# State-space input tables: built by GpSimd in turned layout, beside attention

## The reference, cut to what matters

```python
# attention of the first mixer
p = softmax(concat(q_pos @ keys_lat, q_free @ keys_ctx) * scale)
o = p[..., :s] @ ckv_l + p[..., s:] @ ckv_c          # then @ w_uv, * silu(gate), @ w_out
# state space, one of two directions, 128 groups of 64 complex states and 16 channels
lam_bar = exp(lam * dt)
b_bar = ((lam_bar - 1.0) / lam)[..., None] * bmat
bu = einsum('btgs,gps->btgp', u, b_bar)              # input into the states
h[t] = lam_bar * h[t-1] + bu[t]                      # associative scan
y = einsum('btgp,gsp->btgs', h, cmat).real
# modulation of both blocks
sh, sc, gt = split(silu(c) @ w_mod[i] + b_mod[i], 3)
```

## Time and profile before

| what | value |
|---|---|
| time, median of 3 runs (lowest to highest) | 1574.73 us (1572.53 to 1574.93) |
| the profiled execution, span | 1571.2 us |
| PE busy | 1503.4 us, 96% of the span |
| PEld busy | 1129.3 us, 72% |
| DVE busy | 872.9 us, 56% |
| ACT busy | 402.3 us, 26% |
| POOL busy | 565.2 us, 36% |
| mean granted TensorE clock | 0.993 |

### The profile page before, as it was taken

One profiled execution on the slowest core, in us unless ns is written; L12 is line 12 of the kernel. 1 busy time (PEld: TensorE's weight loads), 2 busy tenths in 40 slices (PEclk: granted clock), 3 DMA queues, 4 the chain that ended last, 5 costly groups with the idle time before them and its releaser, 6 DMA issues.

```text
span 1571.2 us, 25477 instructions
## 1 busy us (share of the span) xinstructions
PE 1503.4 (96%) x10192; PEld 1129.3 (72%) x10192; DVE 872.9 (56%) x1745; ACT 402.3 (26%) x956; POOL 565.2 (36%) x412
## 2 busy tenths in 40 slices
PE   4999989999999999999998999999999999999998
PEld 3455555666655558898877888887788874688887
DVE  5979944554578978378466321243543422265642
ACT  1222243333311222322233011001223550232210
POOL 4013340000002314101002977773496301477774
PEclk9999999999999999999999999999999999999999
DMA  9856771050286646747666455445544133455441
GB/s 332 221 173 194 242 237 45 3 159 14 100 262 228 202 174 180 273 166 287 251 252 260 159 195 182 161 163 185 191 167 146 70 108 107 131 179 164 168 150 68
DMA packets 172605, 272.99 MB, mean 174 GB/s; under 512 B 51405, under 2 KB 85304, under 8 KB 171208
## 3 DMA queue, kind: packets, MB, share of 16 engines
q1 hardware_dynamic: 146096, 201.08, 38.1%
q0 software_dynamic: 16512, 42.49, 8.4%
q10 hardware_dynamic: 9880, 27.78, 4.8%
HBM read 228.26 MB, written 42.99 MB: 173 GB/s over the span
## 4 chain that ended last, share of the span: by engine, by line
PE 88%; DVE 5%; DMA 3%; issue 2%; ACT 2%; POOL 0%; DVEq 0%; ACTq 0%; POOLq 0%
PE bank L499 82%; PE bank L502 6%; DMA memory<-in_w_mod 1%; DMA memory<-mc_scratch 1%; DVE memory L2417 1%; DVE memory L2418 1%; DVE memory L2424 0%; DVE memory L2421 0%; DMA memory<-in_s_log_dt 0%; DVE memory L2574 0%; ACT memory L1514 0%; ACT memory L1386 0%; ACT memory L1738 0%; DVE memory L2445 0%; DVE memory L2444 0%
## 5 line engine op out<-in xcount | busy, mean ns | idle before, releaser
L499 PE MATMUL bank<-memory 128*128 128x256 f32 (+8 forms) x9244 | 1404.7, 355 | 40.4 <-issue 8.5
L499 PEld LDWEIGHTS bank<-memory 128*128 128x128 f32 (+4 forms) x9244 | 1022.3, 166 | 378.1 <-issue 250.1
L2783 POOL DMA_DIRECT2D mc_scratch<-memory x32 | 28.0, 874 | 505.5 <-DVE memory L2138 447.7
L502 PEld LDWEIGHTS bank<-memory 128*128 128x128 f32 (+1 forms) x948 | 109.3, 142 | 59.4 <-issue 33.6
L502 PE MATMUL bank<-memory 128*128 128x128 f32 (+1 forms) x948 | 125.9, 277 | 23.5 <-ACT memory L1358 8.6
L2822 POOL TENSOR_TENSOR memory<-memory 128x1024 f32<-128x1024 f32 (+1 forms) x34 | 80.9, 2378 | 143.5 <-PE bank L499 96.2
L2808 POOL DMA_DIRECT2D memory<-mc_scratch x32 | 17.3, 541 | 189.7 <-PE bank L499 189.7
L2824 POOL TENSOR_TENSOR memory<-memory 128x1024 f32<-128x1024 f32 (+1 forms) x34 | 80.9, 2380 | 2.7
L2789 POOL DMA_DIRECT2D k_scratch<-memory x128 | 76.2, 629 | 14.5 <-ACT memory L1431 14.1
L2827 POOL TENSOR_TENSOR memory<-memory 128x1024 f32<-128x1024 f32 (+1 forms) x34 | 80.0, 2353 | 2.7
L2825 POOL TENSOR_TENSOR memory<-memory 128x1024 f32<-128x1024 f32 (+1 forms) x34 | 80.4, 2366 | 0.0
(11 more groups left out here) (305 smaller groups left out, 1284.3 us busy)
## 6 DMA issues: line engine op xcount, KB each, us to landing
memory<-in_s_w_glu SPq DMA_DIRECT2D x32, 1024.0 KB, 7.5
memory<-in_w_mod SPq DMA_DIRECT2D x12, 2048.0 KB, 14.1
memory<-in_w_ffn_up SPq DMA_DIRECT2D x22, 1024.0 KB, 6.9
memory<-in_w_in SPq DMA_DIRECT2D x10, 2048.0 KB, 8.0
mc_scratch<-memory POOLq DMA_DIRECT2D x32, 512.0 KB, 4.5
mb_scratch<-memory ACTq DMA_DIRECT2D x32, 512.0 KB, 3.7
memory<-mb_scratch SPq DMA_DIRECT2D x32, 512.0 KB, 7.3
memory<-mc_scratch POOLq DMA_DIRECT2D x32, 512.0 KB, 6.5
```

The costliest lines, as they stand in the source:

```text
L499: return nc.tensor.matmul(o, l, r, start=start, stop=stop, skip_group_check=free)
L502: return nc.tensor.transpose(o, i, ident[0:n, 0:n])
L2783: pool.dma_start(mc_dram[u], over(mc[:, u % 3, GS:GS + 1], (144, 8), (1, P))).then_inc(*S.up("mc_out%d" % (u % 3), u, by=16))
```

## The change

1. The input table is no longer made by DVE and transposed by PE. PE transposes the raw `b` once for each quarter (`b_turned`, 4 times 8 transposes), ACT copies and stores it (`bt_scratch`); DVE makes rows of powers once (`power_rows`, some 40 small operations behind unit 2), POOL stores them (`pw_scratch`). Then POOL, for each of the 32 units, loads both spread over the partitions (`pair_load`, three DMAs) and multiplies (`mixed_unit`: two operations of 128x1024, two of 128x512, one store DMA). The unit's complex product is computed in turned layout, so nothing is transposed afterwards.
2. POOL starts once unit 15's output table and the modulation product (0, 5) are done. Its pairs live in ring slot 1; its results in the buffer `gtb` (units 0 to 26) and in the buffer of the probabilities (units 27 to 31, `LAST_MIXED`, after the last head).
3. `gate_rows(0)`, which writes `gtb`, moves behind attention, and on ACT waits for the stores of units 25 and 26.
4. The stores of the output tables and taps move from POOL to ACT.
5. The scaling of the probabilities moves from DVE to ACT (`norm`).
6. The second half of the query weights is loaded right behind the first; the six modulation loads of the second mixer share slot 2, their products stand in heads 8, 9, 11, 12, 14 and 15. The last output weights wait for the last mixed unit. `b` is loaded for all quarters in the gates; quarters 2 and 3 are saved and loaded again (`b_again`).

```diff
-MOD_AT = {3: 0, 5: 1, 10: 2, 12: 3}
+MOD_AT = {8: (1, 0), 9: (1, 1), 11: (1, 2), 12: (1, 3), 14: (1, 4), 15: (1, 5)}
+LAST_MIXED = 5
...
+        pairs = ring[:, 1, :].rearrange("p (a b n) -> p a b n", a=2, b=2)
+        mixed_b = (gtb, hT_flat[:, 0:2048].rearrange("p (a n) -> p a n", a=2))
...
@@ loads @@
+        uq_load(0, 2)
+        uq_load(1, 0)
+        for ct in range(6):
+            mod_load(1, ct, 2)
...
@@ PE @@
-            def unit_turned(u):
-                pe.wait_ge(*S.at("mb", u))
-                for dr in range(2):
-                    b = bank(pe, ("mbT", u, dr), [("mbt", (u, dr))], 4 + dr)
-                    for i in range(4):
-                        last = tr(b[:, i * P:(i + 1) * P], mb[:, u % 2, dr * 512 + i * P:dr * 512 + (i + 1) * P])
-                    last.then_inc(*S.up("mbT_mm", (u, dr)))
-                if u % 2:
-                    kernels(u // 2)
+            def b_turned(q, i):
+                pe.wait_ge(*S.at("b_load%d" % (q % 2), q))
+                for ql in range(2):
+                    b = bank(pe, ("bT", q, ql), [("bT", (q, ql))], i + ql)
+                    for n in range(4):
+                        c = (n % 2) * 512 + (n // 2) * 256 + ql * P
+                        last = tr(b[:, n * P:(n + 1) * P], b_loaded(q)[:, c:c + P])
+                    last.then_inc(*S.up("bT_mm", (q, ql)))
...
             mod_turned(0, 5, 7)
-            gate_rows(0)
-            unit_turned(15)
+            kernels(7)
...
@@ PE, behind the last head @@
-            mod_product(1, 4)
-            mod_product(1, 5)
-            mod_turned(1, 4)
-            mod_turned(1, 5)
+            gate_rows(0)
...
@@ ACT, unit_stored @@
-                for dr in range(2):
-                    act.wait_ge(*S.at("mbT_mm", (u, dr)))
...
-                    A(mbt_(u)[:, dr * 512:(dr + 1) * 512], at_bank("mbT", u, dr), ACT.Copy).then_inc(*S.up("mbt", (u, dr)))
-                act.wait_ge(*S.at("mbt", (u, 1)))
-                act.dma_start(mb_dram[u], mbt_(u)).then_inc(*S.up("mbt_out%d" % (u % 2), u, by=16))
+                act.wait_ge(*S.at("mc", u))
+                act.dma_start(mc_dram[u], over(mc[:, u % 3, GS:GS + 1], (144, 8), (1, P))).then_inc(*S.up("mc_out%d" % (u % 3), u, by=16))
...
+                    for j in range(L):
...
+                        act.dma_start(to, kt[:, kp % 2, (7 - j) * GS:(7 - j) * GS + P]).then_inc(*S.up("k_out%d" % (kp % 2), kp, by=16))
...
@@ ACT, attention @@
+            def norm(h):
+                c = 4 * (h % 2)
+                act.wait_ge(*S.at("inverse", h))
+                for t in range(NTT):
+                    act.wait_ge(*S.at("p", (h, t)))
+                    o = pl[:, h % 2, t, :] if t < 2 else pc[:, h % 2, t - 2, :]
+                    A(o, o, ACT.Copy, scale=st0[:, 56 + c + t:57 + c + t]).then_inc(*S.up("pn", (h, t)))
...
@@ ACT, behind the last head and six DMA issues @@
+            for u in (NU - LAST_MIXED - 2, NU - LAST_MIXED - 1):
+                act.wait_ge(*S.at("mb_out%d" % (u % 2), u))
+            gate_rows(0)
             for ql in range(2):
                 c_conjugated(2, ql)
...
@@ DVE, unit: the six operations of the input table @@
-                tt(o[0], w[0], b[0], ALU.mult).then_inc(*S.up("unit_op", (u, 5)))
...
-                tt(o[1], o[1], t[1], ALU.add).then_inc(*S.up("mb", u))
...
@@ POOL @@
+            def pair_load(u):
+                q, g8 = u // 8, u % 8
+                if u >= 2:
+                    pool.wait_ge(*S.at("mixed", u - 2))
+                b, w = pairs[:, u % 2, 0, :], pairs[:, u % 2, 1, :]
+                pool.dma_start(b, dview(bt_dram, q * P * 8 * P + g8 * GS * 8 * P, (0, 8), (8 * P, GS), (1, 8 * P))).then_inc(*S.up("pair_in%d" % (u % 2), u, by=16))
+                for ql in range(2):
+                    src = dview(pw_dram, (16 * q + 8 * ql + g8) * 4096, (512, 8), (0, GS), (1, 512))
+                    pool.dma_start(w[:, ql * 512:(ql + 1) * 512], src).then_inc(*S.up("pair_in%d" % (u % 2), u, by=16))
+            def mixed_unit(u):
...
+                pool.wait_ge(*S.at("pair_in%d" % (u % 2), u))
+                if u >= 2:
+                    pool.wait_ge(*S.at("mb_out%d" % (u % 2), u - 2))
+                if u == NU - LAST_MIXED:
+                    pool.wait_ge(*S.at("pt_mm", (H - 1, 2)))
+                nc.gpsimd.tensor_tensor(both(o), both(b), both(w, 0, 0), ALU.mult).then_inc(*S.up("mix_op", (u, 0)))
+                pool.wait_ge(*S.at("mix_op", (u, 0)))
+                nc.gpsimd.tensor_tensor(both(w), both(b, P, -P), both(w, P, 0), ALU.mult).then_inc(*S.up("mix_op", (u, 1)))
+                pool.wait_ge(*S.at("mix_op", (u, 1)))
+                nc.gpsimd.tensor_tensor(part(o, 0), part(o, 0), part(w, 0), ALU.subtract).then_inc(*S.up("mix_op", (u, 2)))
+                nc.gpsimd.tensor_tensor(part(o, P), part(o, P), part(w, P), ALU.add).then_inc(*S.up("mixed", u))
+                pool.wait_ge(*S.at("mixed", u))
+                pool.dma_start(mb_dram[u], o).then_inc(*S.up("mb_out%d" % (u % 2), u, by=16))
+            pool.wait_ge(*S.at("mod_mm", (0, 5)))
+            pool.wait_ge(*S.at("mc", 15))
+            pool.wait_ge(*S.at("pw_out"))
+            for u in range(NU + 1):
+                if u < NU:
...
+                    pair_load(u)
+                if u:
+                    mixed_unit(u - 1)
```

255 lines of the change are left out of this document (144 added, 111 removed).

## The result

The changed kernel takes 1670.32 us (median of four runs, 1668.31 to 1679.92), the kernel before 1574.06 us on the same chip. The ratio is 1.0629, with a 95% interval of 1.0600 to 1.0658. Forecast were 1590.5 us and a range of 1548 to 1603: the sign was right, the size was off by 80 us. Of the changed kernel the profiled execution has a span of 1669.3 us, 98.1 us more than before. (Each timed execution is 1.8 us longer than its own span; the forecast had added 3.5.)

A forecast was written before the change was run, and what follows sets the result against it. PE was taken to bound both stages. PE 26.8 us late waiting for POOL, plus 3.0 for the clock, minus 14.0 of transposes gave 15.8 us slower: 1587.0 span, 1590.5 us timed, range 1548 to 1603.

The forecast's parts named there:

- PE bounds, and the transposes are on its path: Gates and output product: PE's work is the chain; 32 transpose groups removed, four added, 24.6 us net saved.
- Scaling on ScalarE, nothing: Attention: ACT takes over the scaling, 2.2 us a head, with nothing waiting except 0 to 1 us in first and last heads.
- Two more modulation products in heads: Attention: two more products of 1.9 us each come into the heads, the same that stood behind.
- `power_rows` beside what DVE no longer does: Gates: some 40 small DVE operations cost nothing, or 15 us if the cover of dropped operations were gone.
- ACT now issues the eight tap stores here, 0.41 us each; I put 0.2 us on the path (bounds 0 and 3.3): End of the gates: 3.3 us of ACT store issues beside 6.5 us of PE work, adding 0.2 us.
- POOL's first operation at 210.7 (206.5 to 214): Start of POOL's units: unit 15 ready at 203.2, first pair landed at 208.8, first operation at 210.7 us.
- A unit, 9.60 us (7.44 to 10.1): POOL's time per unit: 7.44 us of operations plus four DMA issues, 2.16 us.
- Under my forecast all this hides in the 37 us: Attention: late modulation loads (0 to 2.4 us, or 5, three times) cost nothing inside the 37.5 us wait for POOL.
- Rival (c): Attention: modulation loads land late, 0 to 2.4 us or 5, three times; 0.07 on top of POOL in time, 1557 to 1565.
- No window above has DMA near its limit: Argument against other waits filling the transposes' place, a rival of 1571 to 1580 us given a chance of 0.02.
- The hole at the end, 40 us and cold clock behind: Between attention and output product: PE idles some 40 us for POOL's unit 26, then 3.0 us lost to a slower clock.
- -14.0 us in the output product, 11.0 with the 3.0 for the clock: Behind attention: 16 removed transpose groups save 14.0 us, less 3.0 for the slow clock after the hole.

The follow-up runs named there:

- a_taps: The changed kernel with the tap stores of the first eight pairs moved back from ACT to POOL; 1665.7 us (ratio 1.0584).
- b_norm: The kernel before with only the scaling of the probabilities moved from DVE to ACT; 1574.9 us against 1573.6 (ratio 1.0004).
- a_pairs: The changed kernel with each of POOL's pair loads cut to an eighth of its columns; 1624.6 us (ratio 1.0322).
- a_mods: The changed kernel with the six modulation weight loads of attention cut to an eighth; 1652.2 us (ratio 1.0508).
- b_gone_hi: The kernel before with six of each unit's eight transposes left out for units 16 to 31 only; 1561.8 us (ratio 0.9924).

## Why the prediction was wrong

- **PE bounds, and the transposes are on its path: right.** The run without six of every eight shows 17.9 us where the count gives 21. With the tap stores off ACT (a_taps) PE passed the end of the gates at 210.02, for a forecast of 209.9.
- **Scaling on ScalarE, nothing: right** (b_norm).
- **Two more modulation products in heads: right** as products (12.35 us for 10.46), wrong as loads, below.
- **`power_rows` beside what DVE no longer does: nearly right.** They take 15.3 us in one piece (85.8 to 101.1) and PE shows no wait for them.
- **"ACT now issues the eight tap stores here, 0.41 us each; I put 0.2 us on the path (bounds 0 and 3.3)": the first step that failed.** Issues cost 0.62 us each with room and 2.7 us on average at 215. The 0.41 came from two issues of other DMAs in an idle stretch. The bounds said nothing of full queues, though the pairs' first loads were to go out at that very moment. Measured on the path: 18.0 us, and 8.5 and 7.1 at two other places, which I had not looked at. It is the first step that failed, not the dearest: without the first two of these holes the time falls by 5 us only (a_taps), since POOL comes last.
- **POOL's first operation at 210.7 (206.5 to 214): failed.** It came at 233.51. Unit 15 was 9.4 us late, mostly by the first hole (212.56 for the first issue, forecast 203.2). And the first pair landed only then, 19.1 us after the end of its last issue (214.40), not 4.5: I had taken the median landing of a store. POOL stood idle for 17.35 us of it; in a_taps, without ACT's stores beside it, still for 13.8, and in a_pairs, with an eighth of the bytes, for 5.8. The Trainium skill's GPSIMD Engine Reference (2.1, Instruction dispatch) gives the first call of fresh code some 6 us; the wait here ends with the landing, so no run shows such a cost.
- **A unit, 9.60 us (7.44 to 10.1): small error.** 10.08 us. The durations were right to 0.02 us; short by 0.06 us on each issue, start to start, and by the 0.30 us that POOL waits ahead of each store. Over 26 units 12.5 us.
- **No term at all for landings between units: failed, and the dearest step.** Of the 54.2 us, 35.7 fall between the first unit and unit 26, in eight waits. POOL's own term is thus 22.8 (start) + 12.5 + 35.7 + 5.5 left over, of which 3.6 are longer operations: 76.5 us late at the end of unit 26 (544.2 for 467.7). That is what PE meets at the second turned group (75.1 late).
- **"Under my forecast all this hides in the 37 us" (modulation loads): failed in the reasoning.** The hole would have hidden it if POOL had kept its time. But the same traffic delays POOL, so PE's 20.8 us and POOL's 36.9 us come together; a_mods moved both.
- **"No window above has DMA near its limit": the root.** I read the DMA share of the kernel before (0.05 in attention) and not what a unit adds: 1536 KB every 9.6 us, 164 GB/s. A 2048 KB load that lands in 14.1 us is another 149 GB/s; 313 together, where 211 are a share of 0.63, make 0.93. In truth the pairs take more than their bytes say: nearly alone, with the units' stores, they have a share of 0.64 at 158 GB/s, in this window of the changed kernel:

```profile
272.00:292.00 20.00, 19.96 (x86) 12.41 (x86) 8.62 (x16) 9.22 (x22) 19.25 (x16) 1.00 0.64 158
```

Rival (c) had the traffic, but priced it at 0 to 15 us and only for PE.
- **The hole at the end, 40 us and cold clock behind: right in place and cause** (49.8 us; clock 0.54 in the window of the hole, close to the lower level of 1.2 GHz). **The size was luck**: POOL came 76.5 us late and PE 63.4 (493.86 for 430.5), and the hole is what is left between the two errors; in a_taps, with PE 29.9 us earlier, it was 77.2. The prediction had named longer heads as what would make it wrong: four of them held waits for weights, 3.3 to 7.1 us each.
- **-14.0 us in the output product, 11.0 with the 3.0 for the clock: failed.** 3.9 were given back. The 7.1 us that are missing are as long as the hole at 619 behind ACT's stores. The clock was 0.95 from 550 to 600 us, 2.5 us, as forecast; 0.93 from 600 to 650 follows the second hole. The 14.0 themselves hold: b_gone_hi has 11.8 us for twelve groups of sixteen.

## What to carry to other kernels

When a change turns work of a compute engine into memory traffic, add the bytes to the windows it falls into before anything else: the rate per unit, the share that the same rate has in another window, and which loads run beside it. Take the share over the whole stage, not from one window in which no load happens to fall. A DMA issue is priced in a quiet stretch only for quiet stretches; put stores on an engine whose list nobody waits for, and ask what stands behind them there. And price the removed work by itself first: a run without most of the transposes put their gain at little over 1%, less than the new traffic cost.
